# Moving the rope angles, the window means and four middle sums of a fused transformer kernel to other places

## The reference

```python
    h = _rmsnorm(x, ln_mlp_g[l])
    x = x + jnp.square(jax.nn.relu(h @ w_mlp_up[l])) @ w_mlp_down[l]
    ...
    h = x @ w_in
    x_q, x_kv, k_rope_raw, gate_a, u_pool, gate_b = jnp.split(h, splits, axis=-1)
    y_a = mla_branch(x_q, x_kv, k_rope_raw, positions, q_norm_g, w_uq, kv_norm_g, w_ukv) * jax.nn.silu(gate_a)
    y_b = pool_branch(u_pool, pool_w, pool_scale) * jax.nn.silu(gate_b)
```

## Time and profile before

| | us |
|---|---|
| median of 3 runs (2311.07 to 2311.28) | 2311.12 |
| the profiled execution | 2311.61 |
| its span | 2309.8 |
| busy in it: PE / DVE / POOL / ACT | 2239.5 / 1696.6 / 1181.8 / 837.4 |

### The profile page before, as it was taken

One profiled execution on the slowest core, in us unless ns is written; L12 is line 12 of the kernel. 1 busy time (PEld: TensorE's weight loads), 2 busy tenths in 40 slices (PEclk: granted clock), 3 DMA queues, 4 the chain that ended last, 5 costly groups with the idle time before them and its releaser, 6 DMA issues.

```text
span 2309.8 us, 29212 instructions
## 1 busy us (share of the span) xinstructions
PE 2239.5 (97%) x10722; PEld 1852.5 (80%) x10722; DVE 1696.6 (73%) x2041; ACT 837.4 (36%) x1165; POOL 1181.8 (51%) x891
## 2 busy tenths in 40 slices
PE   7999999999999999999999999899999989999998
PEld 5678888888888899887878888788888767779886
DVE  7899999976778454446686666877777874568777
ACT  4312242123333356222443333444343424444423
POOL 3236553333323256334488888899884768400140
PEclk9999999999999999999999999999999999999999
DMA  4121123533332422444244444744433111441231
GB/s 155 37 83 64 64 91 114 166 134 115 110 128 83 128 74 61 156 154 156 103 159 151 151 151 150 296 165 151 150 119 141 55 68 60 127 154 46 67 110 73
DMA packets 93589, 272.50 MB, mean 118 GB/s; under 512 B 8784, under 2 KB 25304, under 8 KB 87064
## 3 DMA queue, kind: packets, MB, share of 16 engines
q1 hardware_dynamic: 76400, 206.34, 26.6%
q10 hardware_dynamic: 17064, 64.51, 7.9%
HBM read 186.13 MB, written 83.90 MB: 117 GB/s over the span
## 4 chain that ended last, share of the span: by engine, by line
PE 88%; DVE 7%; ACT 1%; issue 1%; DMA 1%; SPq 0%; POOL 0%; ACTq 0%; DVEq 0%; POOLq 0%
PE pair L1228 35%; PE pair L1566 25%; PE pair L1591 6%; PE pair L1781 4%; PE pair L1477 3%; PE pair L1750 2%; PE pair L1737 1%; PE pair L1455 1%; PE pair L1397 1%; PE pair L1247 1%; PE pair L1444 1%; PE pair L1446 1%; DVE tsp L2888 1%; PE pair L1726 1%; PE pair L1723 1%
## 5 line engine op out<-in xcount | busy, mean ns | idle before, releaser
L1228 PE MATMUL pair<-actA,w_hi 128*128 128x512 f32 x2016 | 624.3, 391 | 2.7 <-issue 2.1
L1228 PEld LDWEIGHTS pair<-actA,w_hi 128*128 128x128 f32 x2016 | 377.5, 188 | 82.5 <-ACT sq L1919 2.9
L1228 PE MATMUL pair<-actA,w_lo 128*128 128x512 f32 x1008 | 393.1, 390 | 0.0
L1063 POOL TENSOR_TENSOR pad<-pad 128x1 f32<-128x1 f32 x93 | 24.8, 266 | 587.0 <-PE pair L1228 507.9
L1566 PE MATMUL pair<-tring,wsp 128*128 128x512 f32 x1344 | 308.4, 392 | 7.4 <-DVE tring L2961 5.7
L1566 PEld LDWEIGHTS pair<-tring,wsp 128*128 128x128 f32 x1344 | 253.6, 189 | 62.0 <-issue 8.4
L1179 POOL TENSOR_TENSOR wsp<-wraw,wsp 128x512 fp32r<-128x512 f32 x124 | 184.2, 1485 | 87.0 <-ACT wsp L2186 86.5
L1228 PEld LDWEIGHTS pair<-actA,w_lo 128*128 128x128 f32 x1008 | 189.5, 188 | 39.5
L1067 POOL TENSOR_TENSOR w_lo<-raw,w_hi 128x1024 fp32r<-128x1024 f32 (+1 forms) x93 | 207.6, 2233 | 7.4
L2929 DVE TENSOR_TENSOR xB<-pair,xB 128x1024 f32<-128x1024 f32 x112 | 136.4, 1219 | 72.1 <-PE pair L1566 72.0
L1566 PE MATMUL pair<-tsp,wsp 128*128 128x512 f32 x768 | 184.0, 391 | 4.1 <-DVE tsp L2888 2.0
(11 more groups left out here) (450 smaller groups left out, 4519.5 us busy)
## 6 DMA issues: line engine op xcount, KB each, us to landing
wraw<-w_pair SPq DMA_DIRECT2D x41, 1024.0 KB, 6.6
raw<-w_in SPq DMA_DIRECT2D x62, 512.0 KB, 3.5
staged<-hid_d SPq DMA_DIRECT2D x56, 512.0 KB, 3.3
proj<-stage ACTq DMA_DIRECT2D x40, 512.0 KB, 2.6
hid_d<-hsum SPq DMA_DIRECT2D x16, 1024.0 KB, 5.0
gates<-proj ACTq DMA_DIRECT2D x18, 512.0 KB, 5.3
raw<-w_out SPq DMA_DIRECT2D x16, 512.0 KB, 3.5
hid_d<-hid SPq DMA_DIRECT2D x16, 512.0 KB, 2.8
```

What stands on the lines that cost most here:

```text
L1228: last = nc.tensor.matmul(pair[par][:, cols], w[:, slot, wk], x[:, cols], start=(k == 0 and i == 0), stop=(k == kt - 1 and i == 2))
```

## The change

Five things are done.

The angles leave the strips. DVE computes them in 12 pieces (`angle(k)`), one behind P6 and one behind P4 of steps 3 to 8; ACT takes the sines in step 10. Positions, angles and results lie at 104 to 120 KB, where xB's upper half is loaded, so that load moves from the start of the up part to its pair 13, behind the store of cos and sin.

The window means are cut into their doublings (`level`), which stand between the strips' adds.

The last four middle sums stand singly, behind the lo parts of pieces 3 to 6, and SP loads the weights of step 18 ahead of the last store.

The strips come in another order: the first half of gate a goes between the halves of the q latent, its second half behind them, the kv latent last.

The kv latent's squares, mean, root and norm move behind the strips; PE does the mean behind the first query product.

```diff
@@ strips: columns, destinations @@
-            tensor, first = ((u2, 0), (u2, 2), (gb, 0), (gb, 2), (xq, 0), (xq, 2), (xkv, 0), (u2, 0), (u2, 2))[st - STEPS]
+            tensor, first = ((u2, 0), (u2, 2), (gb, 0), (gb, 2), (xq, 0), (u2, 0), (xq, 2), (u2, 2), (xkv, 0))[st - STEPS]
@@ SP @@
-            sp.dma_start(xB[:, 4:8, :], x_d[:, 4:8, :]).then_inc(x_in, 16)
+            sp.dma_start(posi0[:, :], t["pos_row"].partition_broadcast(P)).then_inc(pos_in, 16)
             for u in range(N_PAIR):
+                if u == N_PAIR - 3:
+                    sp.wait_ge(cs_moved, 16)
+                    sp.dma_start(xB[:, 4:8, :], x_d[:, 4:8, :]).then_inc(x_in, 16)
...
                 if at_run == 7 * N_PAIR + 1:
+                    load_pair(N_PAIR + 2)
                     store_rest(N_PAIR - 1)
...
-                if at_run == START[st] + 3 and st + 2 < ALL_STEPS:
+                if at_run == START[st] + 3 and N_PAIR < st < ALL_STEPS - 2:
                     load_pair(st + 2)
@@ PE @@
-                if i == NO[STEPS + 4, "P7"]:
+                if i == NO[STEPS + 5, "P3"]:
                     pe.wait_ge(pooled_ok, 4)
                     pool_product(2)
                     pool_product(3)
-                if i == NO[STEPS + 6, "P3"]:
+                if i == NO[STEPS + 8, "P1"]:
                     latent_mean("xq", "mean512")
-                if i == NO[STEPS + 7, "P3"]:
-                    latent_mean("xkv", "mean256")
...
             product_first(FIRST["uq"], 4, qh, ql, lo_ok, base)
+            latent_mean("xkv", "mean256")
@@ ACT @@
+                if at_run == NO[10, "P2"]:
+                    act.wait_ge(trig_in, 2)
+                    step(nc.scalar.activation(cs0[:, 0, :], cs0[:, 0, :], ACT.Sin))
+                    step(nc.scalar.activation(cs0[:, 1, :], cs0[:, 1, :], ACT.Sin))
+                    act.dma_start(cs_d, cs0[:, :, :]).then_inc(cs_moved, 16)
...
             nc.scalar.copy(kr[:, HALF:S], pair[n % 2][:, 0:HALF]).then_inc(copied, 1)
+            root(("stat", "xkv"), (squares_used, STAT_BASE["xq"] + 2), EPSV, rstd_kv[:, :])
             his(0, [xkv_hi[:, g, :] for g in range(2)], [xkv[:, g, :] for g in range(2)], (nrm, NT + 5))
@@ DVE @@
+                if 3 <= st < 9 and p in ("P6", "P4"):
+                    angle(2 * (st - 3) + (p == "P4"))
-                if p == "P1" and st <= N_PAIR:
-                    unit_sums(st - 1)
+                if p == "P1" and st < N_PAIR:
+                    unit_sums(st - 1, (0, 2, 1, 3))
                 for j in range(N_SPLIT):
                     if T_TURN[j] == i:
                         split_lo(j)
+                if st == N_PAIR and p in ("P5", "P6", "P2", "P7"):
+                    unit_sums(N_PAIR - 1, ({"P5": 0, "P6": 2, "P2": 1, "P7": 3}[p],))
...
+            level(0, 0)
             add_strip(STEPS + 2, "P2")
-            angles()
+            pooled(0)
             add_strip(STEPS + 2, "P7")
-            dve.wait_ge(copied, copies(NO[STEPS + 1, "P4"]))
-            pooled(0)
             add_strip(STEPS + 2, "P3")
-            dve.wait_ge(cs_moved, 16)
+            level(1, 0)
+            level(1, 1)
             pooled(1)
+            level(2, 0)
+            add_strip(STEPS + 3, "P2")
```

More of the change, by code:

```diff
@@ L2274, in copy_strip @@
                 act.wait_ge(mul_done, i + 1)
-                func = ACT.Silu if p == "P4" and st - STEPS in (2, 3, 7, 8) else ACT.Copy
+                func = ACT.Silu if p == "P4" and st - STEPS in (2, 3, 5, 7) else ACT.Copy
                 nc.scalar.activation(strip_out(st, p), half_bank(strip_bank(st, p)), func).then_inc(copied, 1)
@@ L2955, in unit_sums @@
                 t_sums([hid[:, HID_OF[p], :] for p in ("P2", "P3", "P4", "P7")],
-                       [hsum[:, q, :] for q in range(4)], 16 + 4 * u, (0, 2, 1, 3))
+                       [hsum[:, q, :] for q in range(4)], 16 + 4 * u, order)
             def split_lo(j):
@@ L3110, in pooled @@
                 step(V.tensor_tensor(other, src[:, 0:16], cst[:, a:a + 16], ALU.mult))
[L3111 removed]
+                step(V.scalar_tensor_tensor(u2[:, g, 16:S], src[:, 16:S], 1.0 / POOL_WINDOWS[g], u2[:, g, 16:S],
                                             ALU.mult, ALU.subtract))
@@ L3156, in _ @@
             squares_into(sqa, sqb, [xq[:, g, :] for g in range(2)], True)
-            for p in ("P2", "P7", "P3"):
-                add_strip(STEPS + 5, p)
-            dve.wait_ge(copied, copies(NO[STEPS + 5, "P4"]))
-            dve.wait_ge(evicted, adds(NO[STEPS + 5, "P3"]))
-            squares_into(sqa, sqb, [xq[:, g, :] for g in range(2, 4)], False)
+            add_strip(STEPS + 7, "P2")
+            dve.wait_ge(copied, copies(NO[STEPS + 6, "P4"]))
+            dve.wait_ge(evicted, adds(NO[STEPS + 6, "P3"]))
+            squares_into(sqa, sqb, [xq[:, 2, :]], False)
+            add_strip(STEPS + 7, "P7")
+            add_strip(STEPS + 7, "P3")
+            squares_into(sqa, sqb, [xq[:, 3, :]], False)
             V.tensor_copy(tiny[:, 31:32], tiny[:, 30:31]).then_inc(squares, 1)
-            for p in ("P2", "P7", "P3"):
-                add_strip(STEPS + 6, p)
             def norm2(tiles, gain, scale):
@@ L3195, in _ @@
             V.tensor_copy(kr[:, 0:HALF], pair[n % 2][:, 0:HALF]).then_inc(unit_out[n % 2], 1)
+            dve.wait_ge(rstd_ok, 13)
+            norm2([(g, xkv[:, g, :]) for g in range(2)], "kv_norm_2", rstd_kv)
             for g in range(2):
```

171 lines of the change are left out of this document (85 added, 86 removed).

## The result

The changed kernel takes 2316.7 us (median of 9 runs, 2312.71 to 2319.8) against 2310.43 for the kernel before in the same sessions (9 runs, 2307.8 to 2311.28): ratio 1.0026, 95% interval 1.0017 to 1.0035. It is slower by 6 us, more than 0.2%. The forecast was 2310.6, with a range from 2303 to 2316, so the measured median lies just outside.

A forecast was written before the change was run, and what follows sets the result against it. PE, busy 97% of the span, bounds the kernel, so only its stops and slow runs count. T +6, S -13.5 and Q +7 sum to -0.5 us: 2310.6 for the median, 8 in 10 from 2303 to 2316.

The forecast's parts named there:

- S: Strips: stops for DVE's adds go, less a new wait in the first query product; -11.8 to -14.7, taken as -13.5 us.
- T: Turn from MLP up part to down part: late last sum and store delay xB; +3.8 to +7.5, taken as +6 us.
- Q: Query products: late kv root delays the key's first add and rope chain; +4.4 to +7.5, taken as +7 us.
- Angles in the up part: MLP's up part: twelve DVE pieces hidden by 79 us room on DVE and 36 on POOL; 0 us.
- The early load of weights: Turn: step 18's weights asked for 11 us earlier; nothing on PE waited for them, so 0.
- My wait for the third lo part: First query product: q latent's third lo part late behind the kv squares; PE waits 0.5 to 3.4 us.
- The key's first add: Query products: ends about 13 us behind the second product's start, where it ended 2.4 behind it before.
- the fourth remaining product: Query products: waits for a bank behind the rope chain; late by 10.6 us, or 7.5 if DMAs land faster.
- The clock rival: Two stops, at the turn and third query product, each cost a 2.6 us restart; 2316 to 2318; chance 0.18.

The follow-up runs named there:

- b_ang: Kernel before with only angles, their sines, positions' load and load of xB's upper half moved into the up part: 2305.59 us, ratio 0.9977.
- run 115: Not an experiment: a run of 12 PE matmuls in step 16; before the change PE stood 4.95 us ahead of it for piece 3's lo part.
- a_krsq: a_kr with kv squares behind lo parts and the key's copies, kv mean behind the second query product, kv root behind both bank reads: 2308.71 us, ratio 0.9996.
- a_again: The changed kernel once more, unchanged, for a second profile: 2317.43 us, ratio 1.0037.
- b_T: Kernel before with only the turn's edit: single middle sums behind lo parts, early load of step 18's weights: 2318.07 us, ratio 1.0035.
- a_kr: Changed kernel with the rotary key's chain ahead of the kv latent's normalization: 2316.34 us, ratio 1.003.
- a_cs: a_krsq with cos and sin asked for once PE is done with the rope key's product: 2306.27 us, ratio 0.9979.
- a_noT: Changed kernel without the turn's edit: last four middle sums in one block, step 18's weights asked for at the old place: 2309.93 us, ratio 0.9999.
- run 121: Not an experiment: PE matmuls needing the bank that DVE's first add of step 17 frees; stops ahead of it 2.73 and 4.94 us after the change.
- a_noLP: Changed kernel with only the load of step 18's weights back at its old place: 2321.89 us, ratio 1.0056.
- a_two: Changed kernel with the last four middle sums in two pairs, behind lo parts 4 and 5: 2310.91 us, ratio 1.0007.
- a_blockLP: Changed kernel with the last four middle sums in one block, early load of step 18's weights kept: 2309.89 us, ratio 0.9992.
- run 117: Not an experiment: a run of 12 PE matmuls in step 16; PE stood 1.87 us ahead of it in both profiles of the changed kernel.
- run 118: Not an experiment: a run of 12 PE matmuls in step 16; stops ahead of it 3.73 and 2.16 us in the changed kernel's two profiles.

## Why the forecast was wrong

The forecast was -0.5, the measured difference +6.3 in the first comparison and +7.7 in the second. The mechanisms named in it are all in the traces. What failed is a size: S gained too little, because the wait that it held against the strips' gain was priced too low and without a restart. T and Q lie at or just above the upper ends of their ranges and add the rest.

**Angles in the up part, 0: right.** b_ang shows no cost. POOL's busy time grew by 7.2 us for the same 139 instructions between 1200 and 1440, where it had 36 us of room, as forecast. That two-input instructions of DVE hold POOL up is what the Trainium skill's page "SBUF — State Buffer", section "Who interferes with whom", says, and the trace agrees in kind; the 12 to 15 us that I had made of it is more than the 7.2 measured.

**T, +6 (3.8 to 7.5): right in kind, somewhat too small.** Every link is in the trace: no stop ahead of run 115, the last sum ending at 1484.3 (forecast 1482.8 to 1486.5), xB's second load in at about 1496.3 (1494.6 to 1498.3), PE back at 1497.63 (1495.8 to 1499.5); counted from the U of before, each is 1.7 later and still inside. U to V is +4.8 in the first profile, +4.75 in a_krsq, and +6.9 to +7.5 in a_again, b_T, a_kr and a_cs; in the medians T is 7.5 (a_noT) and 8.3 (b_T). Between the two profiles of the changed kernel the difference is the longer landing of the store and the clock: the first restarted run 121 at full clock, the second at 0.50, which I had counted.

**The early load of weights, 0: right for the sum, wrong as a judgement of the edit.** I judged it by the kernel before, where nothing waited for these weights. Behind a late store they become the next wait, and a_noLP puts a price of 5 us on their old place. My T took these weights to be in time, so the error is not in the sum.

**S, -13.5 (-11.8 to -14.7): this step failed.** The strips themselves gained more than I had put down, 17.64 in V to W: 15.2 for the stops and slow runs, 1.3 for the kv mean that moved out (W to M has it), 1.1 that I can't place. But W to M took 9.14 more. My wait for the third lo part was 0.5 to 3.4 us, about 1.7 in the sum, with 2.20 us at most for one instruction of the squares and no term for a restart; it was 4.67 in after, a_again, a_two, a_noLP, a_blockLP and a_kr, 4.65 in a_noT. The squares took 6.5 us from start to end where I had 5.6 at most, as the sum (1977.01, 3.25 us) and the second square (1975.03, 1.94) lay beside POOL's lo part of weights, and the twelve matmuls behind the stop ran at the low clock. By the starts of the rows: twelve matmuls at the full clock end at 1974.08 + 2.72 = 1976.80, the restart is 4.82 later; the mean starts 5.29 behind it, 2.57 more than 2.72; the second product starts 1.75 behind the mean. 4.82 + 2.57 + 1.75 = 9.14. a_krsq, which beyond a_kr moves only squares, mean and root, sets W to M back to 5.44 and takes 7.6 us off the median. S was -8.5 in the first profile and -9.8 to -11.5 in a_kr, a_blockLP, a_two, a_again, a_noLP and a_noT, each against the 220.47 of before; against b_T, whose strips are those of before (219.18), each gain is 1.3 smaller.

**Q, +7 (4.4 to 7.5): right in kind, too small by 1 us, half right in cause.** M to X is +6.3, +5.85 in a_again, against the profile of before. But in b_T and b_ang, whose query products are those of before, M to X is 42.5 and 42.9: the profile of before has 2 us of slow matmuls behind its stop of 2.14 us, where these two come back at the full clock from one of 2.04. Against them Q is +8, and 10.5 to 10.9 in a_noT and a_blockLP, where the rotation fell beside POOL's lo part and took 6.5 us instead of 4.5. The key's first add ended at 2002.4 = M + 13.8 (forecast M + 13), and the fourth remaining product was 8.7 us late (10.6, or 7.5 with faster DMAs). And I held the key's first add for the one cause. a_kr takes it away and wins nothing in M to X: cos and sin, loaded behind the kv latent's last lo part as well, hold the rotation to 2.3 us less, and POOL's work takes most of that. On the table loads the row was the better guide than the page "ScalarE: Activation LUTs", section "What ACT_TABLE_LOAD costs", of the Trainium skill: after the change, Exp again starts 1.30 us behind its load (1990.40 to 1991.70), and no drain stands between.

**The clock rival (2316 to 2318) had the right time for partly the right reason.** It named restarts at the third query product and ahead of runs 117 or 118, 5.2 us. The traces have such restarts: behind the stop ahead of run 117 in a_again (4.57 us), behind the one ahead of run 118 (36 matmuls in 11.05 and 10.05 us, 8.2 at the full clock), at the third query product, and in the first query product, which it did not name. But of the 7.9 to 9.1 us that W to M grew by in the two profiles, 4.8 are the stop, 1.3 the mean and 1.7 to 3.0 the slow matmuls. Against the 1.7 in the sum the stop alone is 3 us too long, which the rival did not have.

**The sum of the measured terms.** Against the one profile of before: T +7.4, S -10.2 (the middle of a_kr, a_blockLP, a_two, a_again and a_noT), Q +6: +3.2, and 3 to 4.5 us would be missing. That profile was itself a long one, 2311.61 where the medians of its kernel are 2309.75 to 2310.93. Against b_T and b_ang where their code is that of before: T +7.2 (309.45), S -8.9, Q +8: +6.3, beside 6.3 and 7.7 measured. The medians say the same from the other side: T alone 8.3, all the rest 0.2 where the forecast had -6.5. These are single profiles, and stretches with the same code differ by up to 2.6 us between them, so a split finer than that stays open.

## What to carry to other kernels

When work is moved out of a full stretch, price it where it lands by the duration that such an instruction has beside the engines that are busy there, and add a restart to a stop that it makes. Before undoing one cause of a late instruction, list all that it waits for: with two chains of nearly equal length, taking one away shows little until the other goes. Take the terms of a sum from more than one execution of the kernel before: here two restarts in its first profile made the gain of S look 1.3 us larger and the price of Q 2 us smaller. A transfer that nothing waits for is free only as long as the transfers ahead of it in its queue keep their time.
